# Two projection chunks moved ahead of their stages, and the turned reads moved within a step

## The reference

```python
u = h * (1.0 + scale[:, None, :]) + shift[:, None, :]
proj = u @ w_in[layer] + b_in[layer]
hy_streams, hy_gate, pool_in, pool_gate = jnp.split(proj, splits, axis=-1)
# hyena branch: short convolution over 3 taps, then two long convolutions
v, x1, x2 = jnp.split(s, HYENA_ORDER + 1, axis=-1)
z = v
for o, g in enumerate((x1, x2)):
    z = g * _bidir_long_conv(z, k_freq[:, o], bias[o])   # rfft, product, irfft over 4096
# pooling branch, then
y = jnp.concatenate([y_h * silu(hy_gate), y_p * silu(pool_gate)], axis=-1)
out = gate[:, None, :] * (y @ w_out[layer] + b_out[layer])
h = _layer_norm(DEEPNORM_ALPHA * h + out, ln_g[layer], ln_b[layer])
```

## Time and profile before

| what | us |
|---|---|
| median of 3 runs | 1323.71 |
| the profiled execution | 1323.71 |
| its span | 1321.9 |
| TensorE busy in the span | 1129.1 |
| VectorE busy | 866.2 |
| ScalarE busy | 534.7 |
| p3, from TensorE's first matmul in it to that of p4 | 567.25 to 746.76 |
| p4 | 746.76 to 885.17 |
| p5, to the first load of the stage behind it | 885.17 to 1051.70 |

### The profile page before, as it was taken

The page is one execution under the profiler, slowest core; times in us unless marked ns, Lnnn a source line. Parts: engine busy times, 40 slices in busy tenths (PEclk is TensorE's granted clock), DMA queues, the critical chain, the costliest instruction groups (busy, mean ns, idle before and its releaser), DMA issues. The chain is left out here.

```text
span 1321.9 us, 14467 instructions
## 1 busy us (share of the span) xinstructions
PE 1129.1 (85%) x4940; PEld 865.8 (65%) x4940; DVE 866.2 (66%) x1068; ACT 534.7 (40%) x721; POOL 151.7 (11%) x98
## 2 busy tenths in 40 slices
PE   4788837899999999979889978998887656899996
PEld 1256725788887877768767755676665434688885
DVE  5968749655555355559889545638878448577776
ACT  2447734434342233327666333325666445211110
POOL 0010034211111112110011110111100014000000
PEclk9879957999999999989999988999999778899999
DMA  8359988587755245579988578768898597622221
GB/s 296 120 195 360 331 235 286 205 266 248 235 182 173 62 124 180 190 188 253 257 246 247 168 222 255 219 199 214 246 272 233 164 361 267 239 96 96 95 95 48
DMA packets 156176, 276.48 MB, mean 209 GB/s; under 512 B 24711, under 2 KB 46215, under 8 KB 153994
## 3 DMA queue, kind: packets, MB, share of 16 engines
q1 hardware_dynamic: 151613, 269.53, 64.5%
q0 software_dynamic: 3168, 5.51, 1.5%
q10 hardware_dynamic: 1328, 0.59, 0.2%
HBM read 183.30 MB, written 98.57 MB: 213 GB/s over the span
## 5 line engine op out<-in xcount | busy, mean ns | idle before, releaser
L150 PE MATMUL prj_pp<-prj_uhi,prj_whi 128*128 128x512 f32 x768 | 311.4, 406 | 12.4 <-POOL prj_ulo L1043 7.4
L152 PE MATMUL prj_pp<-prj_uhi,prj_wlo 128*128 128x512 f32 x768 | 306.0, 398 | 0.0
L151 PE MATMUL prj_pp<-prj_ulo,prj_whi 128*128 128x512 f32 x768 | 306.0, 398 | 0.0
L150 PEld LDWEIGHTS prj_pp<-prj_uhi,prj_whi 128*128 128x128 f32 x768 | 149.1, 194 | 55.3 <-issue 23.4
L151 PEld LDWEIGHTS prj_pp<-prj_ulo,prj_whi 128*128 128x128 f32 x768 | 148.9, 194 | 31.6
L152 PEld LDWEIGHTS prj_pp<-prj_uhi,prj_wlo 128*128 128x128 f32 x768 | 147.9, 193 | 32.9
L150 PE MATMUL out_ps<-whl,out_yhi 128*128 128x512 f32 x256 | 102.3, 400 | 4.6 <-DVE out_ylo L1996 4.6
L151 PE MATMUL out_ps<-whl,out_yhi 128*128 128x512 f32 x256 | 102.1, 399 | 0.0
L152 PE MATMUL out_ps<-whl,out_ylo 128*128 128x512 f32 x256 | 102.1, 399 | 0.0
L679 POOL CAST prj_whi<-prj_ws 128x1024 fp32r<-128x1024 f32 x24 | 28.9, 1203 | 617.8 <-PE prj_pp L152 432.6
L1174 DVE TENSOR_TENSOR p_alo<-p_a,p_ahi 128x1024 fp32r<-128x1024 f32 x32 | 46.0, 1436 | 67.9 <-ACT p_ahi L1107 67.7
(11 more groups left out here) (183 smaller groups left out, 2078.8 us busy)
## 6 DMA issues: line engine op xcount, KB each, us to landing
kseq<-fs_xo SPq DMA_DIRECT2D x32, 512.0 KB, 5.0
p_a<-kseq SPq DMA_DIRECT2D x32, 512.0 KB, 4.4
kfreq<-p_out SPq DMA_DIRECT2D x32, 512.0 KB, 5.2
xseq<-p_xo SPq DMA_DIRECT2D x32, 512.0 KB, 6.8
p_a<-xseq SPq DMA_DIRECT2D x32, 512.0 KB, 6.2
p_k_re<-kfreq SPq DMA_DIRECT2D x64, 256.0 KB, 4.5
p_k_im<-kfreq SPq DMA_DIRECT2D x64, 256.0 KB, 5.3
bseq<-p_out SPq DMA_DIRECT2D x32, 512.0 KB, 5.9
```

The lines of the kernel that those rows point to most:

```text
L150: nc.tensor.matmul(out, w[0], m[0], start=start, stop=False, skip_group_check=True)
L151: nc.tensor.matmul(out, w[0], m[1], start=False, stop=False, skip_group_check=True)
L152: return nc.tensor.matmul(out, w[1], m[0], start=False, stop=stop, skip_group_check=True)
```

## The change

Two things are changed. First, the reads of parts 2 and 3 of a turned tile: in p1 they go from the front of the next step to the end of the tile's own step. In p3 they go from the next step to the own step, between `evac` and `yhigh`; the reads of parts 0 and 1 go behind `to_row`. SP's stores stay where they are. Second, three rows of the plan: p3, p4 and p5 begin one step earlier and have a chunk at step -2. p3 has none at step 17 any more, p4 none at step 11, p5 has one at step 14 and none at 15 and 16. All other slots are the same, and so is the number of chunks in each stage.

```diff
@@ values_and_filters, scalar @@
-                turned = plan.due(plan.turn, step, 1)
-                if turned is not None:
-                    tn.read(act, turned, 2)
-                    tn.read(act, turned, 3)
                 turned = plan.due(plan.turn, step)
...
                     pl.scaled(act, pool_at(step, 2))
+                if turned is not None:
+                    tn.read(act, turned, 2)
+                    tn.read(act, turned, 3)
@@ spectrum_product, scalar @@
-                turned = plan.due(plan.turn, step)
-                if turned is not None:
-                    tn.read(act, turned, 0)
-                    tn.read(act, turned, 1)
                 q = plan.due(plan.out, step)
...
-                turned = plan.due(plan.turn, step, 1)
+                turned = plan.due(plan.turn, step)
+                if turned is not None:
+                    tn.read(act, turned, 0)
+                    tn.read(act, turned, 1)
+                if 0 <= step - 1 < NU:
+                    evac(step - 1)
                 if turned is not None:
                     tn.read(act, turned, 2)
                     tn.read(act, turned, 3)
-                if 0 <= step - 1 < NU:
-                    evac(step - 1)
                 if 0 <= step < NU:
                     yhigh(step)
@@ encoder_layer @@
-                (-1, 18, range(-1, 18)),
-                (-1, 19, [-1, 0, 2, 4, 6, 8, 10, 11, 12, 14, 16, 17, 18]),
-                (-1, 20, [-1, 0, 1, 2, 4, 5, 6, 8, 9, 10, 12, 13, 15, 16]))
+                (-2, 17, range(-2, 17)),
+                (-2, 19, [-2, -1, 0, 2, 4, 6, 8, 10, 12, 14, 16, 17, 18]),
+                (-2, 19, [-2, -1, 0, 1, 2, 4, 5, 6, 8, 9, 10, 12, 13, 14]))
```

## The result

| | before | after |
|---|---|---|
| median, us | 1324.44 (4 runs, 1322.33 to 1326.5) | 1342.53 (4 runs, 1341.64 to 1350.17) |
| ratio, 95% interval | | 1.0149 [1.0109, 1.0191] |
| profiled execution, its span | 1323.71, 1321.9 | 1344.42, 1342.6 |
| p3 | 179.51 | 193.15 |
| p4 | 138.41 | 141.65 |

A forecast was written before the change was run, and what follows sets the result against it. It took TensorE to bound p1, VectorE p3 (p5 alike), and the even-step inverse units p4. p1 0, p3 -0.5, p4 +3.5, p5 -0.2 sum to +2.8 on 1323.71: 1326.5 us, range 1317 to 1336.

The forecast's parts named there:

- D = 5: Net delay of VectorE's chain in p3 from the moved reads: 5 us, bounds 0 and 10.4, upper bound raised to 17.7.
- Part 2: Reads in p3: `yhigh` waits for a store's landing (2.4 us), `ylow` 2.6 us late, 10.4 over four turn steps.
- The absorbed part: Old waits in p3's VectorE chain that vanish while VectorE stands still for the reads: 5.4 us, half of 10.8.
- The price of the splits: Three GpSimd weight splits in p3 falling on other VectorE instructions: up to 7.3 us more, taken as 0.
- Part 1: Reads in p1 moved to the step's end: cost 0, from below 0 and from above 0.5 us.
- Part 3: p3 gets its chunk earlier: nothing lost or gained at the start; with the read delay, p4 starts 0.5 us earlier.
- Part 4: p4: two chunks before `inv(0)` make `inv(2)` 4.9 us late, the freed step returns 1.9; +3.5 in the sum.
- The term of 1.7 for the low clock: p4's start: first chunk's matmuls at the lower clock after TensorE's pause, 1.7 us more (0 to 2.6).
- Part 5: p5: start 1.2 us late, loop 0 (between -1 and +1), end 1.4 gained; together -0.2.
- the third: Rival at p3's turn steps: read wait lands whole and splits collide, +10 us, 1336.5; chance 0.18.
- The second: Rival in p3: the read wait is absorbed, no change, 1322 us as its middle; chance 0.20.
- The first: Rival: cover at the stages' start was missing, so faster, 1315.4 us, or 1319 where half holds; chance 0.24.

The follow-up runs named there:

- plan alone: Only the new plan rows of p3, p4 and p5, ScalarE's reads where they were, against the kernel before: 1328.8 us, ratio 1.0024.
- reads alone: Only the move of ScalarE's reads, with the plan rows of before, against the kernel before: 1341.52 us, ratio 1.0143.
- p3's slots: Only p3's new chunk slots, reads and other plan rows as before, against the kernel before: 1319.49 and 1321.83 us, ratios 0.9971 and 0.9974.

## Why the prediction was wrong, by its steps

VectorE sets p3, as said: p3's growth is in its chain. The three pieces of p3, forecast and measured: start 0 and -0.75; chain D = 5 and 20.41; end -5.5 and -6.02 (12.63 to 6.61); sum -0.5 and +13.64.

**Part 2 is the step that failed**, and in it the landing, taken as 2.4 us from the earlier trace rows. Those rows are stores that something had waited for, and in the kernel before that was only in p1, on an idle queue. In p3 1.5 MB stand ahead of the store at the first three turns and 512 KB at the last, and it takes 5.46 to 6.47 us and 4.04. The four waits of `ylow` are 19.8 us in place of 10.4. The neighbours gave it away: `bseq`, in the same stage and queue, and the loads of p3 take twice as long and more (6.5 us for `bseq` and 5.9 for `k_im`, by their medians in the window from 600 to 640 us of the kernel before). The absorbed part was of the right size: 5.4 taken, 6.3 measured in `alow`. The price of the splits was set at 0 of a bound of 7.3; it is 5.1. GpSimd's rows after:

```profile
625.47 1.29 POOL L679 CAST prj_whi<-prj_ws 128x1024 fp32r<-128x1024 f32 x1 [32.52 <-PE prj_pp L152]
626.84 2.73 POOL L681 TENSOR_TENSOR prj_wlo<-prj_ws,prj_whi 128x1024 fp32r<-128x1024 f32 x1
```

and the cast of before, 0.54 us ahead of the stretched `ylow` of the earlier trace rows:

```profile
626.04 1.52 POOL L679 CAST prj_whi<-prj_ws 128x1024 fp32r<-128x1024 f32 x1 [36.00 <-PE prj_pp L152]
```

and a second stretched instruction of before, at the third split, which the prediction didn't count:

```profile
709.25 2.05 DVE L1527 TENSOR_TENSOR p_alo<-p_a,p_ahi 128x1024 fp32r<-128x1024 f32 x1
```

After, the subtraction starts first (626.84), and `ylow`, from 627.23, ends 1.08 us behind the subtraction's end at 629.57: it has stood for the rest of it and then done its own work (1.22 where nothing overlaps). With the conv piece of 1.41 (0.75 unstretched) this split costs 2.86 us; the three cost 2.86, 2.86 and 2.74 against 0.84, 0.86 and, with the `alow` of 2.05, 1.67 before. Before, `ylow` started in front of the subtraction, and it ended, again, 1.08 us behind the end of the cast (627.56 and 628.64); it was the subtraction that stretched, to 3.26. So the prediction misread that row, and the rule that it set aside holds: the Trainium skill ("SBUF — State Buffer", section "SBUF: two separate sides") says that whichever starts first has the ports for the whole instruction. What a split costs VectorE depends on who comes first, and the stall moved VectorE behind GpSimd: with the plan alone no instruction beside the three splits is longer than 2.06 us, with the reads alone each split has one of 2.77 or 3.41.

In sum 19.8 + 5.1 - 6.3 is 18.6 of the 20.41. The other 1.8 are smaller waits: the conv's for the turn are 2.9 more, others 1.1 less. So the 15.4 us by which D = 5 fell short are 9.4 of landing, 5.1 of splits and 1.8 of small waits, less the 0.9 that was absorbed beyond the 5.4. The upper bound of 10.4 for the read waits fell with the landing, since it was four times a wait worked out with 2.4 us; it was this bound, and not only the cut of the top from 1340 to 1336, that kept 1342.5 out of reach.

**Part 1** was right: from p1's first matmul to p2 the kernels with the reads moved take 241.8 to 243.9 us, those with the reads of before 242.1 to 244.6.

**Part 3** was right: the chunk at the start costs and gains nothing, and without the stall the end gives 4.6 us (8.06 in place of 12.63).

**Part 4** came out in its sum, +3.24 against +3.5, but partly by luck. It had `inv(2)` some 24 us into p4 and that delay of 5.3 us carried on by even steps of 13.8. `inv(2)` came at 22.80 (787.25), 4.3 late against the 18.48 of before; `inv(6)` was late by only 1.7 (47.72 against 46.02), and `inv(10)` by 4.9 (79.87 against 74.95):

```profile
812.17 0.50 PE L150 MATMUL p_zps<-p_xhi,p_itab 128*128 128x512 f32 x1 [1.88 <-DVE p_xlo L1725]
```

```profile
792.78 0.51 PE L150 MATMUL p_zps<-p_xhi,p_itab 128*128 128x512 f32 x1 [1.56 <-DVE p_xlo L1727]
```

(`inv(6)` after, and before.) Why the even steps were 12.5 and 12.4 us first and 15.4 and 16.8 then is open. The freed step gave 1.7 (844.32 to 872.08 is 27.76, before 29.46), forecast 1.9. The term of 1.7 for the low clock was wrong for this run: p4's first chunks ran at a granted clock of 1.00 after 2.17 us of pause. It is not a fixed price, as the windows of p4's first chunks in the plan-only kernel and in that with p3's slots show (the clock is the third number from the end):

```profile
747.50:754.00 6.50, 6.50 (x29) 5.36 (x30) 5.48 (x4) 1.40 (x3) 3.49 (x2) 1.00 0.69 202
```

```profile
745.00:752.00 7.00, 6.97 (x24) 5.63 (x25) 6.46 (x5) 1.75 (x2) 3.46 (x2) 0.76 0.79 211
```

The pauses ahead were 2.14 and 2.13 us long, and only the second was followed by a stretch at the lower level, 1.2 GHz (mean clock 0.76). What decides between them stays open; so does p4 with both rows of the plan, 4.3 us over nine kernels where Part 4 says 3.5.

**Part 5** was right for this run, +0.1 against -0.2, and VectorE's first product came 1.1 later as forecast (13.58 us into the stage against 12.45). Over all kernels p5 took 174.5 to 178.7 with the new row and 174.4 to 177.4 with the old, on average 177.1 and 175.4, so the new row may cost some 1.7 us that this run doesn't show. The two ranges overlap, and no kernel has this row alone, so that isn't shown.

Of the rivals, the third (the read wait lands whole and splits collide, 1336.5) named the mechanism, with 0.18; it too was worked out with the landing of 2.4, so even it was 6 us too low. The second, that the wait is absorbed, held for 6.3 of 19.8 us. The first, that cover at the start was missing, is refuted: the plan alone is not faster, and what p3's slots gain alone is the end of the stage.

## What to carry to other kernels

Before a wait for a store is put in front of an engine that can't pass it, take the landing from transfers of the same stage and place in the queue, and look at what is issued ahead of it, from all queues; a landing that someone waited for elsewhere is the landing of another load. If the wait must be there, issue the store ahead of the step's loads and put what the critical engine needs ahead of the waiting instruction: here the two together took back 14.8 of the 16.4 us that the reads cost p3 (193.15 to 178.37, with 176.77 for the plan alone). And a stall on one engine shifts its phase to the others: what shared a port harmlessly before may collide after.

## What was not expected of the hardware

A store of 256 KB landed after 2.25 us with nothing ahead, after 4.0 to 4.1 with 512 KB ahead and after 5.4 to 6.8 with 1.5 MB, and an empty queue of its own did not make it faster (5.86 to 6.69). A `ylow` of VectorE that met a GpSimd split, both reading f32 from SBUF, ended 1.08 us behind the GpSimd instruction that had started first; 3.42 us for a `ylow` of 1.22 was the worst. `straight`, one of whose inputs is TensorE's result `p_u`, was not stretched beside the subtraction that ran from 627.64 to 630.90 before (1.29 for its two at 628.73, as without a split at 609.67). And pauses of TensorE of the same length, 2.13 and 2.14 us, were followed by a stretch at the lower clock once and by full speed once.
